# Output projection of a hybrid decoder step: low parts of the last column quarter between the additions, one-column sums between the products of the next group

## The chip, the cores and the metric

The kernel runs on one core of one Trainium2 chip. The metric is the time on the device in microseconds (us). Three runs of the kernel before gave 1358.76, 1359.56 and 1365.93 us; the median is 1359.56 us.

## The reference

One layer of a decoder works on 1088 token columns (1024 of a prompt, 64 of samples) with a width of 1024. A mixer makes two halves of 512 channels, attention heads `a` and gated groups `g`. Then:

```python
merged = concatenate([rmsnorm(a, out_norm_mla_g), rmsnorm(g, out_norm_gmlp_g)])
x = x + merged @ w_out                                   # the output projection
h2 = rmsnorm(x, norm2_g)                                 # needs the sum of x*x of each token
x = x + (silu(h2 @ w_gate) * (h2 @ w_up)) @ w_down
y = rmsnorm(x, final_norm_g)
```

All of it is in float32.

## The kernel before

Channels lie on the 128 partitions and tokens in the free dimension. Every float32 product is made of three products of rounded parts: an operand is split into a high part (`wH`, `mH`) and a low part (`wL`, `mL`, the rest), and `mm3` issues high x high, high x low and low x high (L983, L984, L985) into one PSUM accumulation.

The output projection has 16 steps i. Step i below 8 makes one block of 128 output channels for the first half of the tokens, and i from 8 for the second half; a half has two column quarters of 272 tokens. A pair (step i, column quarter c) is called a group here, and `OUT_STEPS` numbers the 32 groups by q. Group q takes 8 blocks of the contraction, so 24 products of 272 columns, into PSUM bank q % 4. Groups 0 to 15 are column quarters 0 and 1, group 16 is (8, quarter 2), group 17 is (8, quarter 3), and so on.

Who does what, each engine in the order written in its own block, tied by semaphores:

- TensorE makes the groups. From q = 4 it waits for `w_free`, the count of additions, to be q - 3 (addition q - 4 has emptied the bank), and it waits for the split of weight piece i. At group 16 it waits for all low parts (`m_lo`).
- VectorE makes the low parts `mL` of each column quarter (`mixed_low`, L2446), and adds group q to x (`add_rows`, L2458), called addition q here. Each addition waits for its group (`w_ready`) and for the x rows to be loaded. The low parts of quarter 3 (eight instructions) stand as one block between additions 3 and 4.
- ScalarE makes the high parts `mH`, and squares the new x rows (`square4`, L1879).
- GpSimd splits weight piece i (L760 the high, L763 the low part) once the group two steps back is done, and adds the squares up in `sqa` (L790). Between pieces 9 and 10 it takes the power for the factors of the first half of the tokens (L936).
- SyncE issues the transfers in one queue: weight pieces (`raw`, two buffers), x rows (`x2`; the first two loads reuse space and wait for low parts 2 and 4 of the last quarter, L632 and L634), the stores of finished x rows, and the first gate and up weights (`gate_up`, L639) with steps 8 to 11.

The sum of squares over the channels is made on TensorE with the squares as weights and a column of ones as the moving operand (`row_sums`, L1377): 6 blocks of token columns, 2 sources, and two passes for float32 operands, so 24 matmuls of one column. They stand as one clump behind group 16. VectorE makes means of them (`row_means`, L2498), GpSimd the power, VectorE diagonals (L2527), and behind group 18 TensorE spreads the factors over the partitions (L1409), which VectorE then multiplies into x (L2082).

Of the kernel before, what the change touches and what calls it, by code (L numbers as in the profile page):

```python
# [26 lines left out]
P = 128  # L27
# [5 lines left out]
KD = D // P  # L33
# [7 lines left out]
KG = GW // P  # L41
# [35 lines left out]
HALF, SUB = T // 2, T // 4  # L77
# [4 lines left out]
ADDED_1, ADDED_2 = KD - 2, 2 * KD - 5  # L82
# [20 lines left out]
def mixed_order(c):  # L103

    return MIXED if c < 3 else range(2 * KG)
# [17 lines left out]
def offsets(n):  # L123

    return [*range(0, n - P + 1, P)] + ([n - P] if n % P else [])
# [43 lines left out]
def build(nc, d):  # L169
    ctx = ExitStack()  # L170
    with ctx:
# [16 lines left out]
        ones = small.put("ones", [P, P])  # L188
# [124 lines left out]
        sqa, sqb = reg.put("sqa", [P, HALF]), reg.put("sqb", [P, 2, HALF])  # L313
# [35 lines left out]
        ps = ctx.enter_context(nc.psum_tensor("ps", [P, 8, 512], F32))  # L349
# [5 lines left out]
        def sem(name):  # L355
            return ctx.enter_context(nc.semaphore(name))
# [14 lines left out]
        nm_sq, nm_sum, nm_pick, nm_mean, nm_pow, nm_diag, nm_spread = (  # L371
            sem("nm_" + n) for n in ("sq", "sum", "pick", "mean", "pow", "diag", "spread"))
# [29 lines left out]
        m_hi, m_lo, w_ready, w_free = sem("m_hi"), sem("m_lo"), sem("w_ready"), sem("w_free")  # L402
        n4_sq, n4_added, rs_x = sem("n4_sq"), sem("n4_added"), sem("rs_x")
# [48 lines left out]
        def weights_of(t):  # L452

            k = t % TURNS
            return aHL[t % RING] if t < LAST else aHL[(LAST + k) % RING] if k < RING else aHL[k]
# [59 lines left out]
        def _(sp_):  # L515
# [96 lines left out]
            def out_piece(i):  # L612
                piece(N_OUT + i, d["w_out"][ROWS_OUT[i % KD]])

            def load_rows(j, cols=slice(0, T)):
                done = ld_uv_x if cols.start else ld_x[j]
                sp_.dma_start(x2[:, 2 * j:2 * j + 2, cols], d["x"][:, 2 * j:2 * j + 2, cols]).then_inc(done, 16)

            def keep_rows(i, c0, n, q, done):

                m = ROWS_OUT[i % KD]
                sp_.wait_ge(w_free, q + 1)
                sp_.dma_start(x2s[:, m, c0:c0 + n], x2[:, m, c0:c0 + n]).then_inc(done, 16)
# [13 lines left out]
            def gate_up(i, b):  # L637
                src = d["w_gu"][bass.ds(4 * i + b, 1), :, :].rearrange("a p n -> (a p) n")
                sp_.dma_start(wraw[:, b, :], src).then_inc(ff_full[b], 16)  # L639

            for i in range(4, 2 * KD):
                if i >= 6:
                    out_piece(i)
                if i in (6, 7):
                    load_rows(i - 6, slice(HALF, T))
                elif 8 <= i < 12:
                    gate_up(0, (2, 3, 0, 1)[i - 8])
                j = i - 4
                keep_rows(j, HALF * (j // KD), HALF, 2 * j + 1, x2_out[j // KD])
# [330 lines left out]
        def _(pe):  # L980
            def mm3(out, wh, wl, xh, xl, start, stop):

                nc.tensor.matmul(out, wh, xh, start=start, stop=False)  # L983
                nc.tensor.matmul(out, wh, xl, start=False, stop=False)  # L984
                return nc.tensor.matmul(out, wl, xh, start=False, stop=stop)  # L985
# [20 lines left out]
            for t in range(NT):  # L1006
# [4 lines left out]
                for k in range(KD):  # L1011
                    if t == 0 and k % 2 == 0:
                        pe.wait_ge(split_lo, N_V + k // 2 + 1)
                    if (c := {0: 0, 1: 1, 3: 2, 6: 3}.get(t)) is not None:

                        pe.wait_ge(n1_lo, KD * c + k + 1)
                    last = mm3(ps[0:m, b, :], hH[:, k, cols], hL[:, k, cols], vwH[:, k, :], vwL[:, k, :],
                               k == 0, k == KD - 1)
# [37 lines left out]
            for t in range(NT):  # L1056
# [7 lines left out]
                for k in range(KD):  # L1064
                    if t == 0 and k % 2 == 0:
                        pe.wait_ge(split_lo, N_U + k // 2 + 1)
                    last = mm3(ps[0:m, b, :], hH[:, k, cols], hL[:, k, cols], uwH[:, k, :], uwL[:, k, :],
                               k == 0, k == KD - 1)
# [11 lines left out]
            for m in range(KQ + KC + 1):  # L1080
                pe.wait_ge(split_lo, N_IN + m + 1)
                s = m % 2
                for c, (c0, n) in enumerate(CH):
                    q = NC * m + c
                    if q >= 4:
                        pe.wait_ge(z_free, q - 3)
                    for k in range(KD):
                        w = slice(P * k, P * k + P)
                        last = mm3(ps[:, q % 4, 0:n], wH[s][:, w], wL[s][:, w], hH[:, k, c0:c0 + n],
                                   hL[:, k, c0:c0 + n], k == 0, k == KD - 1)  # L1090
# [274 lines left out]
            for h in range(H):  # L1365
                out = ps[VH * (h % 2):VH * (h % 2) + VH, 2, NS * (h // 2):NS * (h // 2) + NS]
                for r in range(KC):
                    last = nc.tensor.matmul(out, uvr[:, r, VH * h:VH * h + VH], olat[:, r, NS * h:NS * h + NS],
                                            start=r == 0, stop=r == KC - 1)
            last.then_inc(a4, 1)  # L1370


            def row_sums(g, bank, sources, at):

                for i, o in enumerate(at):
                    for x, src in enumerate(sources):
                        last = nc.tensor.matmul(ps[:, bank, 500 + i:501 + i], src[:, o:o + P], ones[:, 0:1],  # L1377
                                                start=x == 0, stop=x == len(sources) - 1)
                last.then_inc(nm_sum, 1)

            for q, (i, c) in enumerate(OUT_STEPS):
                s = i % 2
                pe.wait_ge(split_lo, N_OUT + i + 1)
                if q >= 4:
                    pe.wait_ge(w_free, q - 3)
                elif q == 1:
                    sum_squares(J_N3 + NC - 1, 6, sqm, KG, CH[NC - 1][1])
                elif q == 2:
                    pe.wait_ge(a4_e, 1)
                elif q == 3:  # L1390
                    spread(J_N3 + NC - 1, 6, CH[NC - 1][1])
                if q == 2 * KD:
                    pe.wait_ge(m_lo, 2 * KG * 4)
                for j, k in enumerate(mixed_order(c)):
                    if i == 0:
                        pe.wait_ge(m_lo, 2 * KG * c + j + 1)
                    w, cols = slice(P * k, P * k + P), slice(SUB * c, SUB * c + SUB)
                    last = mm3(ps[:, q % 4, 0:SUB], wH[s][:, w], wL[s][:, w], mH[:, k, cols], mL[:, k, cols],
                               j == 0, j == 2 * KG - 1)
                last.then_inc(w_ready, 1)  # L1400
                if q == 2 * KD:
                    pe.wait_ge(n4_sq, KD)
                    pe.wait_ge(n4_added, ADDED_1)
                    row_sums(0, 4, (sqa[:, :], sqb[:, 1, :]), [SUB * x + o for x in range(2) for o in offsets(SUB)])
                elif q == 2 * KD + 2:
                    pe.wait_ge(nm_diag, J_N4 + 1)
                    for x in range(2):
                        for j, o in enumerate(offsets(SUB)):
                            last = nc.tensor.matmul(ps[:, 4 + x, o:o + P], ones[:, :], diag4[:, 3 * x + j, :],  # L1409
                                                    start=True, stop=True)  # L1410
                    last.then_inc(nm_spread, 1)
                elif q == len(OUT_STEPS) - 2:
                    pe.wait_ge(n4_sq, 2 * KD)
                    pe.wait_ge(n4_added, ADDED_2 + 1)
                    row_sums(1, 6, (sqa[:, :], sqb[:, 1, :]), offsets(SUB))
# [102 lines left out]
            for t in range(STEPS):  # L1518
# [13 lines left out]
                w, x = weights_of(t), bHL[t % RING]  # L1532
                for o in range(KH):
# [9 lines left out]
                    for s in range(2) if p < M7 else (p - M7,):  # L1543
                        cols = slice(SUB * s, SUB * s + SUB) if p < M7 else slice(0, SUB)
                        last = mm3(ps[:, 2 * o + s, 0:SUB], w[:, 0, at], w[:, 1, at], x[:, 0, cols], x[:, 1, cols],
                                   k == 0, k == TURNS - 1)
# [4 lines left out]
            for o in range(KH):  # L1551
                pe.wait_ge(n5_t, o + 1)
                for i, c in enumerate(offsets(SUB)):
                    if o == 0:
                        pe.wait_ge(y_last, KH + i + 1)
                        nc.tensor.matmul(ps[:, 1 + 2 * i, 500:501], sqy[:, 0, SUB + c:SUB + c + P], ones[:, 0:1],
                                         start=True, stop=False)
                    last = nc.tensor.matmul(ps[:, 1 + 2 * i, 500:501], sqt[:, 1, o, c:c + P], ones[:, 0:1],
                                            start=False, stop=o == KH - 1)
# [519 lines left out]
        def _(dve):  # L2079
# [80 lines left out]
            for t in range(NT + 1):  # L2160
# [17 lines left out]
                if t >= 1:  # L2178
                    w = t - 1
                    m, x = rows(w), v_tile(w)  # L2180
# [258 lines left out]
            def mixed_low(c, js):  # L2439

                cols = slice(SUB * c, SUB * c + SUB)
                for j in js:
                    k = mixed_order(c)[j]
                    x, gain = (aT, g_mla) if k < KG else (gT, g_gmlp)
                    dve.wait_ge(m_hi, 2 * KG * c + j + 1)
                    nc.vector.scalar_tensor_tensor(mL[:, k, cols], x[:, k % KG, cols], gain[:, k % KG:k % KG + 1],  # L2446
                                                   mH[:, k, cols], ALU.mult, ALU.subtract).then_inc(m_lo, 1)

            def add_rows(q):

                i, c = OUT_STEPS[q]
                m = ROWS_OUT[i % KD]
                x = x2[:, m, SUB * c:SUB * c + SUB]
                dve.wait_ge(ld_x[m // 2], 32)
                if m < KH and c >= 2:
                    dve.wait_ge(ld_uv_x, 48)
                dve.wait_ge(w_ready, q + 1)
                nc.vector.tensor_tensor(x, x, ps[:, q % 4, 0:SUB], ALU.add).then_inc(w_free, 1)  # L2458
# [8 lines left out]
            mixed_low(2, range(KG, 2 * KG))  # L2467
            add_rows(2)
            add_rows(3)
            mixed_low(3, range(2 * KG))  # L2470
            for q in range(4, 2 * KD + 1):
                add_rows(q)

            def weight_sums(i):

# [495 lines left out]
```

## Time and profile before

| | |
|---|---|
| median of the runs | 1359.56 us |
| profiled execution | 1362.44 us |
| its span, first to last instruction | 1360.7 us |
| TensorE busy | 1308.5 us, 96% |
| VectorE busy | 821.2 us, 60% |
| ScalarE busy | 513.0 us, 38% |
| GpSimd busy | 429.2 us, 32% |
| mean granted clock of TensorE | 0.986 |

PE is TensorE (PEld its weight loads), DVE is VectorE, ACT ScalarE, POOL GpSimd, SPq the queue of SyncE. A granted clock of 1.00 is 2.4 GHz, 0.50 is 1.2 GHz. The output projection stands at 514 to 628 us of the span. A row of the order of time gives start, duration, engine, line, operation, out<-in with shapes, the count of merged instructions, and in brackets how long the engine had been idle and who released it.

### The profile page before, as it was taken

The page shows a single profiled execution, that of the slowest core. Times are in us where ns is not written, and L with a number is a line of the kernel's source. Part 1 is how long each engine was busy: PE and PEld are TensorE (multiplying, and loading weights), DVE is VectorE, ACT ScalarE, POOL GpSimd, SP SyncE. Part 2 cuts the span into 40 slices and gives each one's busy share as a digit, 9 for nine tenths or more (in the row PEclk, how much of TensorE's full clock was granted, in tenths as well). Part 3 has the DMA queues.
Part 4 walks back from the last instruction along what each step waited for, and adds up shares of the span by engine and source line. Part 5 has one row for each costly group of instructions (what it writes and reads, how often), then busy time and mean ns, then how long its engine had stood idle before and what let it go on. Part 6 is the DMA issues. An engine that isn't in the chain of part 4 may idle for free.

```text
span 1360.7 us, 23850 instructions
## 1 busy us (share of the span) xinstructions
PE 1308.5 (96%) x9362; PEld 1226.2 (90%) x9362; DVE 821.2 (60%) x1241; ACT 513.0 (38%) x902; POOL 429.2 (32%) x279
## 2 busy tenths in 40 slices
PE   6999999999999998999999999999999999999997
PEld 4788988888888558999899999999999999999987
DVE  4874056666666338167944553445535468899976
ACT  5423224566566414113422222222222234444451
POOL 2633335442433115652044444444443400000000
PEclk9999999999999899899999999999999999999998
DMA  8421101000015444641212222122222189757503
GB/s 286 160 60 31 36 17 58 20 17 5 16 66 191 155 163 155 222 133 49 67 69 80 79 74 83 63 79 79 86 73 74 68 304 339 259 189 246 173 1 131
DMA packets 70345, 151.58 MB, mean 111 GB/s; under 512 B 9106, under 2 KB 16658, under 8 KB 69810
## 3 DMA queue, kind: packets, MB, share of 16 engines
q1 hardware_dynamic: 70258, 150.39, 32.4%
q8 instruction: 58, 0.95, 0.3%
q14 instruction: 29, 0.24, 0.1%
HBM read 127.80 MB, written 22.56 MB: 111 GB/s over the span
## 4 chain that ended last, share of the span: by engine, by line
PE 80%; DVE 8%; issue 5%; DMA 3%; ACT 2%; POOL 2%; SPq 0%; POOLq 0%; DVEq 0%; ACTq 0%
PE ps L983 24%; PE ps L984 24%; PE ps L985 24%; PE ps L1199 2%; DMA araw<-in_w_dn 2%; PE ps L1265 1%; DVE x L2082 1%; PE ps L991 1%; DMA ab<-acts 1%; PE ps L1310 1%; POOL rt L782 1%; DVE mL L2446 1%; DVE hL L2136 1%; PE ps L1275 1%; DVE aHL L2757 0%
## 5 line engine op out<-in xcount | busy, mean ns | idle before, releaser
L952 POOL TENSOR_TENSOR ws<-wraw,ws 128x1024 fp32r<-128x1024 f32 x50 | 125.2, 2504 | 215.8 <-ACT ws L1568 215.8
L983 PE MATMUL ps<-bHL,aHL 128*128 128x272 f32 x616 | 178.7, 290 | 6.3 <-DVE bHL L2760 6.1
L985 PE MATMUL ps<-bHL,aHL 128*128 128x272 f32 x616 | 177.3, 288 | 0.0
L984 PE MATMUL ps<-bHL,aHL 128*128 128x272 f32 x616 | 177.2, 288 | 0.0
L2603 DVE TENSOR_TENSOR bufP<-bufP,ps 128x544 f32<-128x544 f32 x66 | 47.4, 721 | 133.7 <-PE ps L985 131.4
L1568 ACT ACTIVATE ws<-wraw 128x1024 fp32r<-128x1024 f32 x55 | 58.4, 1061 | 174.2 <-PE ps L985 168.9
L983 PEld LDWEIGHTS ps<-bHL,aHL 128*128 128x128 f32 x616 | 116.0, 188 | 8.1 <-DVE bHL L2760 8.0
L984 PEld LDWEIGHTS ps<-bHL,aHL 128*128 128x128 f32 x616 | 116.0, 188 | 0.0
L985 PEld LDWEIGHTS ps<-bHL,aHL 128*128 128x128 f32 x616 | 116.0, 188 | 0.0
L975 POOL TENSOR_TENSOR rt<-ms,mhalf 128x3 f32<-128x3 f32 (+1 forms) x3 | 3.0, 998 | 255.1 <-DVE ms L2790 255.1
L2336 DVE TENSOR_TENSOR pTL<-ps,pTH 128x512 fp32r<-128x512 f32 (+1 forms) x96 | 53.2, 555 | 44.3 <-ACT pTH L1568 43.4
L1568 ACT ACTIVATE aHL<-araw 128x512 fp32r<-128x512 f32 x66 | 41.7, 632 | 99.4 <-PE ps L985 57.4
L952 POOL TENSOR_TENSOR ws<-wsum,ws 128x1024 fp32r<-128x1024 f32 x20 | 57.2, 2859 | 61.1 <-ACT ws L1568 61.1
L892 POOL TENSOR_TENSOR prob<-prob,rsm 128x128 f32<-128x128 f32 (+5 forms) x48 | 49.6, 1040 | 78.4 <-DVE rsm L2311 78.4
L2603 DVE TENSOR_TENSOR bufC<-bufP,ps 128x544 f32<-128x544 f32 x42 | 30.2, 720 | 70.0 <-PE ps L985 70.0
L1568 ACT ACTIVATE pTH<-ps 128x512 fp32r<-128x512 f32 (+1 forms) x96 | 46.8, 489 | 50.0 <-PE ps L1199 49.1
L1736 ACT ACTIVATE prob<-ps,nmx 128x128 f32<-128x128 f32 (+3 forms) x64 | 47.3, 740 | 24.1 <-DVE nmx L2322 23.9
L2322 DVE TENSOR_REDUCE nmx<-ps 128x1 f32<-128x128 f32 (+3 forms) x64 | 47.7, 751 | 12.7 <-PE ps L1180 12.2
L1199 PE MATMUL ps<-ident,prob 128*128 128x128 f32 x288 | 49.9, 285 | 3.0 <-DVE pTL L2336 1.8
L983 PE MATMUL ps<-x1H,ws 128*128 128x272 f32 x176 | 50.8, 288 | 2.1 <-POOL ws L952 2.1
L983 PE MATMUL ps<-x5H,ws 128*128 128x272 f32 x176 | 50.9, 289 | 1.9 <-DVE x5L L2518 1.6
L983 PE MATMUL ps<-x3H,ws 128*128 128x272 f32 x176 | 50.9, 289 | 0.9 <-DVE x3L L2513 0.9
(371 smaller groups left out, 4521.3 us busy)
## 6 DMA issues: line engine op xcount, KB each, us to landing
araw<-in_w_dn SPq DMA_DIRECT2D x121, 256.0 KB, 3.6
wraw<-in_w_gu SPq DMA_DIRECT2D x44, 512.0 KB, 3.5
cp<-in_cache SPq DMA_DIRECT2D x64, 272.0 KB, 4.5
ab<-acts SPq DMA_DIRECT2D x34, 272.0 KB, 4.5
raw<-in_w_out SPq DMA_DIRECT2D x16, 512.0 KB, 4.1
acts<-bufC SPq DMA_DIRECT2D x22, 272.0 KB, 2.1
xt<-in_x_tok SPq DMA_DIRECT2D x9, 512.0 KB, 6.7
x<-x2s SPq DMA_DIRECT2D x8, 544.0 KB, 6.1
```

The costliest lines, as they stand in the source:

```text
L782: pool.tensor_tensor(rt[:, j % 4, :], ms[:, j % 4, :], mhalf[:, :].broadcast_to((P, 3)), ALU.pow).then_inc(nm_pow, 1)
L892: pool.tensor_tensor(row, row, rsm[:, r % 4:r % 4 + 1].broadcast_to((P, n)), ALU.mult).then_inc(s_pn, 1)
L952: pool.tensor_tensor(w[:, 1, :], w_source(j), w[:, 0, :], ALU.subtract).then_inc(cw_lo, 1)
L983: nc.tensor.matmul(out, wh, xh, start=start, stop=False)
L984: nc.tensor.matmul(out, wh, xl, start=False, stop=False)
L985: return nc.tensor.matmul(out, wl, xh, start=False, stop=stop)
L1199: last = nc.tensor.transpose(ps[:, 4 + x % 2, P * qi:P * qi + P], prob[:, at:at + P], ident[:, :])
L1568: return nc.scalar.activation(out, x, ACT.Copy, scale=scale)
L1736: nc.scalar.activation(prob[:, prob_at(qt):prob_at(qt) + n], psf[:, 1024 * (r % 2):1024 * (r % 2) + n], ACT.Exp, bias=nmx[:, s:s + 1], sca ...
L2322: nc.vector.tensor_reduce(nmx[:, s], psf[:, at:at + P * (qt + 1)], AX.X, ALU.max, negate=True).then_inc(s_nm, 1)
L2336: nc.vector.tensor_tensor(pTL[:, x % 4, c0:512], ps[:, 4 + x % 2, c0:512], pTH[:, x % 4, c0:512], ALU.subtract).then_inc(t_free, 1)
L2603: nc.vector.tensor_tensor(halves(out[:, g, :]), halves(x[:, g, :]), pair(b + 2 * g), ALU.add).then_inc(added, 1)
```

## The change

The eight low parts of quarter 3 are dealt out: two behind addition 4, two behind addition 5, one each behind additions 6, 7, 8 and 9. SyncE gets a wait for all low parts before each of the gate and up loads of steps 8 to 11. The 24 one-column matmuls, behind group 16 before, are issued in group 17: behind each of the first six of its eight contraction blocks (three products each) come the four matmuls of one token block. The spreading matmuls move from behind group 18 to behind group 19.

```diff
@@ SyncE @@
                 elif 8 <= i < 12:
+                    sp_.wait_ge(m_lo, 2 * KG * 4)
                     gate_up(0, (2, 3, 0, 1)[i - 8])
@@ TensorE @@
+            def row_sum(bank, sources, i, o):
+
+                for x, src in enumerate(sources):
+                    last = nc.tensor.matmul(ps[:, bank, 500 + i:501 + i], src[:, o:o + P], ones[:, 0:1],
+                                            start=x == 0, stop=x == len(sources) - 1)
+                return last
+
             def row_sums(g, bank, sources, at):
 
                 for i, o in enumerate(at):
-                    for x, src in enumerate(sources):
-                        last = nc.tensor.matmul(ps[:, bank, 500 + i:501 + i], src[:, o:o + P], ones[:, 0:1],
-                                                start=x == 0, stop=x == len(sources) - 1)
+                    last = row_sum(bank, sources, i, o)
                 last.then_inc(nm_sum, 1)
+
+            half_at = [SUB * x + o for x in range(2) for o in offsets(SUB)]
...
                     last = mm3(ps[:, q % 4, 0:SUB], wH[s][:, w], wL[s][:, w], mH[:, k, cols], mL[:, k, cols],
                                j == 0, j == 2 * KG - 1)
+                    if q == 2 * KD + 1 and j < len(half_at):
+                        if j == 0:
+                            pe.wait_ge(n4_sq, KD)
+                            pe.wait_ge(n4_added, ADDED_1)
+                        summed = row_sum(4, (sqa[:, :], sqb[:, 1, :]), j, half_at[j])
+                        if j == len(half_at) - 1:
+                            summed.then_inc(nm_sum, 1)
                 last.then_inc(w_ready, 1)
-                if q == 2 * KD:
-                    pe.wait_ge(n4_sq, KD)
-                    pe.wait_ge(n4_added, ADDED_1)
-                    row_sums(0, 4, (sqa[:, :], sqb[:, 1, :]), [SUB * x + o for x in range(2) for o in offsets(SUB)])
-                elif q == 2 * KD + 2:
+                if q == 2 * KD + 3:
                     pe.wait_ge(nm_diag, J_N4 + 1)
@@ VectorE @@
             add_rows(3)
-            mixed_low(3, range(2 * KG))
             for q in range(4, 2 * KD + 1):
                 add_rows(q)
+                mixed_low(3, {4: (0, 1), 5: (2, 3), 6: (4,), 7: (5,), 8: (6,), 9: (7,)}.get(q, ()))
```

## Rows read from the trace of the kernel before

**Rows 1.** The page: busy time of TensorE among the engines, granted clock in 40 slices.

```profile
PE 1308.5 (96%) x9362; PEld 1226.2 (90%) x9362; DVE 821.2 (60%) x1241; ACT 513.0 (38%) x902; POOL 429.2 (32%) x279
...
PEclk9999999999999899899999999999999999999998
```

**Rows 2.** Waits between 510 and 650: us in total, times, longest.

```profile
PE ps L983 <- DVE x L2458: 4.5, 1, 4.5
```

**Rows 3.** TensorE in order of time, around the border of groups 7 and 8.

```profile
541.51 0.29 PE L985 MATMUL ps<-mH,w1L 128*128 128x272 f32 x1
546.26 0.57 PE L983 MATMUL ps<-mH,w0H 128*128 128x272 f32 x1 [4.46 <-DVE x L2458]
```

**Rows 4.** VectorE in order of time.

```profile
535.47 5.78 DVE L2446 SCALAR_TENSOR_TENSOR mL<-aT,g_mla,mH 128x272 fp32r<-128x272 f32 x4
541.18 4.59 DVE L2446 SCALAR_TENSOR_TENSOR mL<-gT,g_gmlp,mH 128x272 fp32r<-128x272 f32 x4
545.69 1.47 DVE L2458 TENSOR_TENSOR x<-x,ps 128x272 f32<-128x272 f32 x4
552.15 0.44 DVE L2458 TENSOR_TENSOR x<-x,ps 128x272 f32<-128x272 f32 x1 [4.99 <-PE ps L985]
555.21 0.44 DVE L2458 TENSOR_TENSOR x<-x,ps 128x272 f32<-128x272 f32 x1 [2.62 <-PE ps L985]
...
576.39 0.44 DVE L2458 TENSOR_TENSOR x<-x,ps 128x272 f32<-128x272 f32 x1 [2.60 <-PE ps L985]
...
583.59 0.44 DVE L2458 TENSOR_TENSOR x<-x,ps 128x272 f32<-128x272 f32 x1 [4.53 <-PE ps L985]
...
591.29 2.85 DVE L2082 SCALAR_TENSOR_TENSOR x<-x,g,ps 128x544 f32<-128x544 f32 x4
```

**Rows 5.** Stretches: length, busy time (instructions) by engine, TensorE's clock, DMA share, GB/s.

```profile
541.50:546.30 4.80, 0.34 (x4) 0.14 (x2) 4.80 (x6) 0.00 (x0) 3.50 (x2) 0.88 0.82 246
546.30:552.00 5.70, 5.70 (x25) 5.70 (x26) 0.86 (x3) 1.32 (x2) 2.68 (x2) 0.50 1.02 399
552.00:576.00 24.00, 24.00 (x193) 24.00 (x191) 3.50 (x8) 2.63 (x4) 16.88 (x11) 1.00 0.54 181
576.10:578.70 2.60, 2.60 (x26) 2.60 (x25) 0.44 (x1) 0.00 (x0) 0.75 (x1) 1.00 0.29 73
578.70:583.20 4.50, 4.50 (x26) 4.50 (x25) 0.17 (x1) 0.00 (x0) 1.34 (x1) 0.62 0.69 264
583.20:586.20 3.00, 3.00 (x26) 3.00 (x25) 1.83 (x2) 0.66 (x1) 2.54 (x2) 1.00 0.00 0
...
497.40:500.80 3.40, 2.63 (x21) 2.22 (x19) 1.92 (x4) 1.17 (x4) 0.00 (x0) 1.00 0.00 0
```

**Rows 6.** TensorE in order of time, start and end of the clump.

```profile
576.12 0.28 PE L1377 MATMUL ps<-ones,sqa 128*128 128x1 f32 x2
...
578.72 0.37 PE L983 MATMUL ps<-mH,w0H 128*128 128x272 f32 x1
578.93 0.29 PE L984 MATMUL ps<-mL,w0H 128*128 128x272 f32 x1
```

**Rows 7.** The line of the one-column sums: ns minimum/median/maximum, first and last start.

```profile
L1377 PEld LDWEIGHTS ps<-ones,sqa x24: 187/192/193, 576.0 to 631.5; 128*128 128x128 f32 x24
L1377 PE MATMUL ps<-ones,sqa x24: 164/250/251, 576.1 to 631.5; 128*128 128x1 f32 x24
```

**Rows 8.** Low parts between 530 and 550, same columns.

```profile
L2446 DVE SCALAR_TENSOR_TENSOR mL<-aT,g_mla,mH x8: 487/895/2628, 531.1 to 539.7; 128x272 fp32r<-128x272 f32 x8
```

**Rows 9.** SyncE's queue in order of time, and landing time of the pieces.

```profile
541.28 0.37 SPq L617 DMA_DIRECT2D x<-in_x  x1
...
542.91 0.48 SPq L520 DMA_DIRECT2D raw<-in_w_out  x1
...
raw<-in_w_out SPq DMA_DIRECT2D x9, 512.0 KB, 4.0
```

**Rows 10.** GpSimd in order of time.

```profile
543.07 2.40 POOL L763 TENSOR_TENSOR w1L<-raw,w1H 128x1024 fp32r<-128x1024 f32 x1
...
579.14 1.34 POOL L936 TENSOR_TENSOR rt<-ms,mhalf 128x6 f32<-128x6 f32 x1 [2.29 <-DVE ms L2498]
```

## Prediction

> **What bounds the kernel now.** I read the busy table and the clock line first. TensorE is busy 96% of the span and its clock stands at 9 tenths or more in every slice, with an 8 at slice 16 [rows 1]: time is won only where TensorE stands still, works at the lower clock, or does something other than 272-column products. The waits of the output projection come next. TensorE waits once there, 4.5 us, for an addition of VectorE [rows 2]; everywhere else VectorE waits for TensorE. The order of time on TensorE shows the place: the last product of group 7 starts at 541.51, the first of group 8 at 546.26 [rows 3]. VectorE's order gives the cause. Between 535.47 and 545.77 it makes the eight low parts of the last column quarter, and only behind them, at 545.69, the addition that frees group 8's bank, though group 4, which it adds, had ended some 13 us earlier (541.6 less three groups of 3.03, worked out below) [rows 3, 4]. Last I cut the time into stretches with the clock. After the standstill TensorE makes 25 products in 5.70 us at granted clock 0.50 (1.2 GHz), where in 552 to 576 it makes 193 in 24 us at 1.00 (2.4 GHz) [rows 5]. A second such place is the clump of one-column sums behind group 16: during it the clock is 1.00, in the 4.50 us behind it 0.62 [rows 5]. So each of the two edits meets one place where TensorE first does little and then pays in clock.
>
> **A normal group.** Additions 9 and 16 start at 555.21 and 576.39: seven groups in 21.18 us, 3.03 us each, 0.126 us for each of its 24 products [rows 4]. An addition starts 0.27 us behind the moment at which the next matmul would start (576.12 to 576.39) [rows 4, 6].
>
> **Edit 1, the low parts dealt out.** Removed: the standstill. Group 8 could start at 541.51 + 0.13 = 541.64 and starts at 546.26: 4.62 us [rows 3]. Its own length, from first product to addition 8, is 552.15 - 546.26 = 5.89 us where 3.03 + 0.27 = 3.30 would do: 2.59 us for the low clock [rows 3, 4]. Together 7.21 us. No instruction is added on TensorE or VectorE; the same eight low parts and additions 4 to 9 come in another order.
> Is the cover there? A low part takes 0.49 us alone and up to 2.63 us [rows 8], the last of them beside GpSimd's subtraction of 543.07 to 545.47 [rows 10]. An addition, which reads PSUM, took 0.44 us at 583.59 [rows 4], in a stretch where GpSimd worked [rows 5]. With addition 4 at 535.5, two lows reach 537.1, addition 5 ends near 537.5, lows 2 and 3 near 541.2, addition 6 near 541.6, low 4 and addition 7 (its group ends 541.6) near 542.5. Group 9 needs addition 5 at 544.7, group 10 addition 6 at 547.7, group 11 addition 7 at 550.7: 5 to 8 us of room, more than the worst low. Low 7 comes after addition 9, near 549, and group 16 needs it at 566. The Trainium skill's page "SBUF — State Buffer" (its part on engine ports) states that VectorE and GpSimd lock a shared pair of ports for a whole instruction when VectorE has two SBUF inputs; the rows of long lows agree. By it the additions, with one PSUM input, are not held up; were they, each would be up to 2.6 us late, still inside that room.
> SyncE's queue: its two loads of x rows wait for low parts 2 and 4. The second was issued at 541.28, just behind the fourth low, and the weight piece 6 behind it at 542.91 [rows 9]. Both lows keep their times within 0.5 us by the order above, since only two additions of about 0.4 us slip in while GpSimd is what holds the lows. What is late next: piece 6 lands 4.0 us after issue at the median [rows 9], at 547; I allow 1.5 more, 548.4, since the transfers are dense there [rows 5]. GpSimd splits it in about 3.5 us (a copy and a subtraction of 2.40 [rows 10]) from the end of group 9, now 547.7, and may have 2.8 us of square additions ahead (two of about 1.4), until 548.3. That ends near 551.9, and group 12 needs it at 553.7: about 2 us of room. Piece 5 is split by 545.47 [rows 10], group 10 needs it at 547.7. The new wait of SyncE for all low parts, ahead of the first gate piece, stands behind piece 8, which itself waits for split 6 at 551.9; the last low is there by 549. Nothing. So edit 1 gives 7.2 us; its bounds are 4.6 (clock still falls) and 7.2, less 2.6 if one low part more than shown delays piece 6.
>
> **Edit 2, the sums dealt out.** The clump is 24 matmuls (six sums, two sources, two passes each). From its first start to the second product behind it 578.93 - 576.12 = 2.81 us, less one product 2.68 us, 0.112 each [rows 6]. Additions 16 and 17 lie 7.20 us apart [rows 4]; 7.20 - 3.03 - 2.68 leaves 1.49 us, the lower clock behind the clump, 0.62 in the mean of 4.5 us [rows 5]. What does dealing do to the 2.68? A one-column matmul is over at once, what takes the time is its weight load (0.192 us each, overlapping [rows 7]). A load can lie beneath a running 272-column product, but those products have loads of their own. If every third is followed by the four matmuls of a sum, one of the five loads from it to the next product lies beneath it, as one does at the clump's start, and four are bare: 24 bare loads as before, 2.68 us. Lower bound: 48 loads of 0.108 us ((578.72 - 576.12)/24) back to back are 5.2 us against 3.03, so 2.15. Upper bound: each load and matmul one after the other, 24 x (0.192 + 0.250) = 10.6 [rows 7]. I take 2.68: the same 24 instructions in the clump row are nearest.
> And the clock? Dealt out, a stretch holds three products of 0.126 and four bare loads, 0.83 us in all, nearly half of it products. The trace has a poorer stretch that kept 1.00: 497.4 to 500.8, with 21 matmuls in 3.4 us and TensorE busy for 2.63 of them [rows 5]. So I expect 1.00 and the 1.49 us won. Bounds 0 and 1.49.
> The rest of the edit: the sums are done near the sixth of eight products' rounds, about 0.8 us before group 17 ends. VectorE's means take some 0.2, GpSimd's power 1.34 us [rows 10]; it ends some 0.8 us after group 17, and GpSimd's split 10 starts that much later. It ended 2.9 us ahead of need before; about 2 are left. The diagonals on VectorE (some 1.5 us) finish near 2.3 us after group 17, the spreading matmuls now stand behind group 19, 6 us after group 17. They cost what they did, some 1.3 us, in another place. VectorE's scaling started at 591.29 [rows 4], behind addition 19; now group 19 ends those 1.3 us sooner and the spread follows it, so the scaling's start against group 20 is unchanged within 0.3 us. ScalarE's square 8 waits for the sums' count and for addition 17; the latter stays last.
>
> **The sum.** 7.21 + 1.49 = 8.70 us. Does it come through to the end? What follows hangs on local events (spread, bank, split), each moved with TensorE; between additions 21 and 31 VectorE is busy most of the time, but from the scaling on, which moves too. The profiled execution took 1362.44 us, its span 1360.7: 1353.7 for it. The median of the runs shown, 1359.56, is 2.9 us less than that execution. The low-clock terms (2.59 + 1.49) are the ones most likely to be smaller in another execution, since the kernel has only a few such stretches; I assign them about half of the 2.9 as absent in the median run, so the change finds 7.2 there: 1352.4.
>
> **Rivals.**
> (a) The wait moves: a low part slips, load and piece 6 come later, and group 12 waits for GpSimd's split. One low of 2.63 us too many takes away some 0.6 to 2.6 us: about 1354.5. For it: GpSimd keeps the lows at 2.6; against: 2 us of room. Chance 0.12.
> (b) The clock falls in group 17 all the same: the 1.49 is not won, and the thinner group takes longer; 1354 to 1355. For it: the clump did it; against: the poorer stretch at 1.00. Chance 0.12.
> (c) The dealt loads hide. The Trainium skill's "TensorE: Matmul & The Clock Gate" (Part 2, step 1) says that TensorE pulls weight loads ahead beneath running matmuls. Worked out from the rows, as a mechanism of this kernel: loads back to back set group 17 to 5.2 us, the sums cost 2.15 and the time is 0.5 us lower, 1351.9. The page by itself would let one expect more, all 2.68; the rows' load spacing does not. Chance 0.08.
> (d) Slower: alternating one-column and 272-column products makes each load and each matmul wait for the other. At 0.44 us for each of 24 this is 10.6 us, 7.9 more than now, which eats edit 1; if this thin filling also drops the clock through groups 17 to 19 (three times 2.4 us), the time is 1359.56 - 7.2 + 7.9 + 7.2 = 1367.5. Without the clock it decides from (2.68 + 7.2)/24 = 0.41 us per dealt matmul. For it: the sums' operands are of another type than the products', and the order changes over six times instead of once; against: at the clump's borders, the same alternation, the spacing shows 0.21 against 0.13 only once [rows 6]. Chance 0.02.
>
> **How the numbers follow.** Forecast 0.66, 1352.4. The range takes the terms' bounds: low 1349.5 (all 8.7 on the median and a little more), high 1356.5 (standstill gone alone, with part of it turned into a wait for the split). 0.5%, what a measurement can tell from no change, is 6.8 us: 1352.8. The forecast lies just below that, so it splits 0.47 to 0.19; (c) counts as faster, (a) and (b) mostly as within. Faster 0.56, within 0.42, slower 0.02.
>
> **What would show it.** TensorE's order: group 8 directly behind group 7, no wait of 4.5 us, clock 1.00 from 541 to 548. Additions 16 to 17 about 5.7 us apart, 24 one-column matmuls in six clusters of four with 0.112 us between, clock 1.00 behind. VectorE: low parts in pairs between additions 4 and 6. Wrong would be a wait of TensorE for GpSimd's split at groups 10 or 12, the clock at 0.50 in group 18, or the additions 16 and 17 more than 6.5 us apart.

## Result and profile after

| | before | changed |
|---|---|---|
| median | 1359.16 us (8 runs) | 1352.63 us (8 runs) |
| lowest to highest | 1357.11 to 1365.93 us | 1348.71 to 1354.30 us |
| profiled execution, its span | 1362.44, 1360.7 us | 1352.70, 1351.0 us |

The ratio is 0.9938, 95% interval 0.9917 to 0.9959: faster by 6.5 us at the medians. The forecast was 1352.4 us.

The page after, against [rows 1]. The slice of 544 to 578, at 0.8 before, is at 0.9 now; TensorE is busy 3.5 us less and makes as many instructions.

```profile
PE 1305.0 (97%) x9362; PEld 1222.5 (90%) x9362; DVE 823.8 (61%) x1241; ACT 513.4 (38%) x902; POOL 428.5 (32%) x279
...
PEclk9999999999999899999999999999999999999998
```

TensorE in order of time at the border of groups 7 and 8, against [rows 3]: 4.75 us from start to start there, 0.13 now. The wait of [rows 2] has gone; no wait of TensorE for an addition is left in this stage.

```profile
539.97 0.29 PE L986 MATMUL ps<-mH,w1L 128*128 128x272 f32 x1
540.10 0.29 PE L984 MATMUL ps<-mH,w0H 128*128 128x272 f32 x1
```

VectorE in order of time, against [rows 4]. Additions 2, 3 and 4 stand together from 533.24, and the low parts come behind the additions 4 to 9, one or two each; additions 16 and 17 are 5.68 us apart, not 7.20.

```profile
533.24 1.12 DVE L2469 TENSOR_TENSOR x<-x,ps 128x272 f32<-128x272 f32 x3
534.29 1.69 DVE L2457 SCALAR_TENSOR_TENSOR mL<-aT,g_mla,mH 128x272 fp32r<-128x272 f32 x2
535.90 0.42 DVE L2469 TENSOR_TENSOR x<-x,ps 128x272 f32<-128x272 f32 x1
...
539.97 0.42 DVE L2469 TENSOR_TENSOR x<-x,ps 128x272 f32<-128x272 f32 x1
...
546.80 0.51 DVE L2457 SCALAR_TENSOR_TENSOR mL<-gT,g_gmlp,mH 128x272 fp32r<-128x272 f32 x1
...
567.63 0.44 DVE L2469 TENSOR_TENSOR x<-x,ps 128x272 f32<-128x272 f32 x1 [2.60 <-PE ps L986]
572.39 0.17 DVE L2509 TENSOR_SCALAR ms<-ps 128x6 f32<-128x6 f32 x1 [4.32 <-PE ps L1377]
573.31 0.44 DVE L2469 TENSOR_TENSOR x<-x,ps 128x272 f32<-128x272 f32 x1 [0.76 <-PE ps L986]
...
580.59 2.86 DVE L2093 SCALAR_TENSOR_TENSOR x<-x,g,ps 128x544 f32<-128x544 f32 x4 [0.83 <-PE ps L1420]
583.70 0.44 DVE L2469 TENSOR_TENSOR x<-x,ps 128x272 f32<-128x272 f32 x1 [0.25 <-PE ps L986]
```

Group 17 on TensorE, its first two rounds. A round is one contraction block with its four one-column matmuls; it takes 0.82 us (568.10 to 568.92).

```profile
567.73 0.28 PE L1377 MATMUL ps<-ones,sqa 128*128 128x1 f32 x2
567.87 0.36 PE L1377 MATMUL ps<-ones,sqb 128*128 128x1 f32 x2
568.10 0.37 PE L984 MATMUL ps<-mH,w0H 128*128 128x272 f32 x1
...
568.92 0.37 PE L984 MATMUL ps<-mH,w0H 128*128 128x272 f32 x1
```

Stretches after, columns as in [rows 5]: the former standstill, group 17 with its sums, and what follows. The clock is 1.00 in all three.

```profile
540.00:547.00 7.00, 7.00 (x58) 7.00 (x57) 6.34 (x9) 0.69 (x2) 6.42 (x4) 1.00 0.82 273
...
567.70:573.20 5.50, 5.50 (x49) 5.50 (x48) 0.53 (x2) 0.00 (x0) 0.98 (x2) 1.00 0.61 178
573.20:579.00 5.80, 5.80 (x49) 5.80 (x48) 2.67 (x3) 0.66 (x1) 4.77 (x3) 1.00 0.16 63
```

**Where the 9.7 us between the two spans come from.** Before the changed region 1.5 us: additions 2 and 3 started at 534.77, now at 533.24, after a shorter stretch of low clock near 235 which has nothing to do with the change. In the region 8.8 us: addition 20 moved from 594.06 to 583.70, 10.36 us less the 1.53. After it 0.7 us go back: there is a stretch at 0.50 from 678.0 to 681.4 that the profile before does not have, while TensorE waits 0.9 us less for `bHL` (5.2 us against 6.1).

```profile
678.00:681.40 3.40, 3.40 (x17) 3.40 (x17) 2.06 (x2) 0.00 (x0) 0.69 (x1) 0.50 0.00 0
```

So 8.8 us in these two executions, where the sum said 8.70. The medians over all executions show 6.5.

### The profile page after: what moved, and what is told of

It reads as the page before. It is cut to its first block, busy times and chain, and to the rows that moved or that the text cites. A ratio compares the mean times of both kernels' runs of the same rounds, so it can differ in the third digit from the quotient of the medians.

```text
span 1351.0 us, 23850 instructions
## 1 busy us (share of the span) xinstructions
PE 1305.0 (97%) x9362; PEld 1222.5 (90%) x9362; DVE 823.8 (61%) x1241; ACT 513.4 (38%) x902; POOL 428.5 (32%) x279
## 4 chain that ended last, share of the span: by engine, by line
PE 81%; DVE 8%; issue 5%; DMA 3%; ACT 2%; POOL 1%; SPq 0%; POOLq 0%; DVEq 0%; ACTq 0%
PE ps L984 24%; PE ps L985 24%; PE ps L986 24%; PE ps L1200 2%; DMA araw<-in_w_dn 1%; PE ps L1266 1%; DVE x L2093 1%; PE ps L992 1%; DMA ab<-acts 1%; PE ps L1311 1%; POOL rt L783 1%; DVE hL L2147 1%; PE ps L1276 1%; DVE aHL L2768 0%; DVE bHL L2771 0%
```

## Experiments

Theory: each edit takes away its own place; edit 1 the standstill and the low clock behind it, edit 2 only the low clock behind the clump, since the sums' weight loads cost the same wherever they stand. Rivals: all the gain lies in one edit; the dealt loads hide; changes between the two kinds of matmul cost.

**e1, edit 1 alone** (on the kernel before):

```diff
                 elif 8 <= i < 12:
+                    sp_.wait_ge(m_lo, 2 * KG * 4)
...
-            mixed_low(3, range(2 * KG))
...
                 add_rows(q)
+                mixed_low(3, {4: (0, 1), 5: (2, 3), 6: (4,), 7: (5,), 8: (6,), 9: (7,)}.get(q, ()))
```

> The kernel before with edit 1 alone (low parts dealt out, the extra wait of SyncE). Theory (each edit removes its own place): no wait of TensorE before group 8, clock 1.00 there; additions 16 and 17 stay 7.2 us apart if the clock falls behind the clump, 5.7 if it does not; time 4.6 to 7.2 us below before, ratio 0.9947 to 0.9966. Rival A (all gain is in the low parts, dealing the sums brings nothing): as fast as the changed kernel, 0.994. Rival B (the wait moves to GpSimd's split of piece 6): TensorE waits at group 12 and the gain is under 4.6.

Measured: 1354.16 us, ratio 0.9941 (0.9918 to 0.9965). No wait before group 8. The clump is followed by the low clock, and additions 16 and 17 lie 7.21 us apart (569.47 to 576.68). Stretches of this profile:

```profile
572.60:576.00 3.40, 3.40 (x17) 3.40 (x16) 0.00 (x0) 0.00 (x0) 0.96 (x1) 0.50 0.76 290
541.00:548.00 7.00, 7.00 (x57) 7.00 (x56) 6.63 (x7) 0.66 (x1) 6.17 (x5) 1.00 0.73 226
```

Edit 1 carries most of the gain: 5.4 us at the medians. Rival B is out. Rival A cannot be told from the theory by the time (1.3 us above the median of the changed kernel in e0, with overlapping intervals); the 7.21 us speak against it.

**e2, edit 2 alone:** the sums and the spread as changed, the low parts as one block as before, without SyncE's new wait.

> The kernel before with edit 2 alone (sums dealt out in group 17). Theory: the standstill of 4.6 us before group 8 and the low clock behind it stay; additions 16 and 17 are 5.7 us apart, clock 1.00 behind; time 0 to 1.5 us below before (ratio 0.9989 to 1.0), depending on whether the clump would have pulled the clock down. Rival (dealing costs something of its own): slower than before by 0.5 us or more.

Measured: 1357.30 us, ratio 0.9978 (0.9959 to 0.9996). The standstill is there, 4.46 us; additions 16 and 17 are 5.69 us apart. The rival, a cost of dealing, is out. At the medians it is 2.3 us, more than the expected 0 to 1.5; the interval takes in both. Where the clock stays up, dealing itself is worth next to nothing: from addition 16 to addition 20 this profile has 16.07 us (572.50 to 588.57), and the kernel before in e7, below, with its clump, 16.11 (572.47 to 588.58).

**e7 and e9, the kernel before again**, one profile each.

> The kernel before once more, for its profile. Theory (what follows a standstill or a clump in clock is not the same in every execution): the standstill before group 8 is 4.6 us again; the low clock behind it is there for 3 to 7 us; the low clock behind the clump may be missing, then additions 16 and 17 are 5.7 apart. Rival (fixed costs): both as in the first profile, 5.9 us from first product of group 8 to addition 8 and 7.2 us between additions 16 and 17.

> The kernel before a third time, for its profile. Two profiles of before and the one with the low parts alone showed the clump of sums: additions 16 and 17 lay 7.20 and 7.21 us apart with a stretch at 0.50 behind the clump, and 5.65 without one. Theory: one of these two values again, and for the standstill an addition 8 that comes 5.9 or 5.0 us behind the first product of group 8. Rival: values in between.

Measured, one run each: 1356.83 us and 1361.06 us. The standstill was 4.46 us in both. VectorE in e7, additions 16 and 17 around the means:

```profile
572.47 0.44 DVE L2458 TENSOR_TENSOR x<-x,ps 128x272 f32<-128x272 f32 x1 [2.60 <-PE ps L985]
574.97 0.17 DVE L2498 TENSOR_SCALAR ms<-ps 128x6 f32<-128x6 f32 x1 [2.06 <-PE ps L1377]
578.12 0.44 DVE L2458 TENSOR_TENSOR x<-x,ps 128x272 f32<-128x272 f32 x1 [2.98 <-PE ps L985]
```

The two additions are 5.65 us apart, with the clump in its old place. The clock was 1.00 during and behind it in this execution:

```profile
543.40:546.60 3.20, 3.20 (x14) 3.20 (x15) 0.89 (x3) 1.32 (x2) 2.10 (x2) 0.50 1.04 412
...
572.20:574.80 2.60, 2.60 (x27) 2.60 (x25) 0.44 (x1) 0.00 (x0) 0.73 (x1) 1.00 0.31 72
574.80:578.00 3.20, 3.20 (x28) 3.20 (x28) 0.17 (x1) 0.00 (x0) 1.34 (x1) 1.00 0.95 350
```

What the clock costs in each profile: the time from the first product of group 8 to addition 8 less 3.30 us, and from addition 16 to 17 less 5.68. The last column is the length of a stretch at 0.50 that every profile has between 436 and 452, long before the changed region:

| profile | group 8 to addition 8 | cost | additions 16 to 17 | cost | early stretch |
|---|---|---|---|---|---|
| before, first | 5.89 | 2.59 | 7.20 | 1.5 | 10.2 |
| before, e7 | 4.84 | 1.54 | 5.65 | 0.0 | 3.4 |
| before, e9 | 5.86 | 2.56 | 7.20 | 1.5 | 10.2 |
| e1, edit 1 alone | no standstill | 0 | 7.21 | 1.5 | 10.2 |
| e2, edit 2 alone | 4.85 | 1.55 | 5.69 | 0.0 | 3.4 |
| changed | no standstill | 0 | 5.68 | 0 | 10.2 |
| e0, changed again | no standstill | 0 | 5.68 | 0 | 3.4 |

The values fall on two levels, as the theory had it. The standstill is fixed, what follows in clock is not. Of four profiles with the clump the clock fell behind it in three, and the levels go with the early stretch: the higher costs stand where it was 10.2 us long. So e0 and e2, with the short one, say little on whether dealing keeps the clock up, since it stayed up in e7 too. The changed kernel's first profile says more: its early stretch is the long one, and the clock stayed up, and so it did with the long one in e3, e5, e6 and e8 below.

**e0, the changed kernel again,** beside e1 to e3.

> The changed kernel itself once more, on the chip and beside the runs of the experiments. Theory and rivals alike: ratio to before 0.9938 within 0.002. Its stretches at the lower clock: those at 234 and 439 again, none at 541 to 548 and none behind group 17; one at 678 may or may not be there.

Measured: 1352.84 us, ratio 0.9936 (0.9915 to 0.9957), profiled span 1347.6 us. As expected at 541 to 548 and behind group 17; the stretch at 678 was missing. The early ones were at 232.7 to 239.5 and 447.7 to 451.1, not quite "234 and 439".

**e3, the block one addition later:**

```diff
-                mixed_low(3, {4: (0, 1), 5: (2, 3), 6: (4,), 7: (5,), 8: (6,), 9: (7,)}.get(q, ()))
+                mixed_low(3, range(2 * KG) if q == 4 else ())
```

> The changed kernel, but all eight low parts of quarter 3 stand as one block, behind addition 4 instead of before it. Theory (only addition 4 was late, for group 8): the block of some 10 us ends near 543.5, addition 5 comes near 543.6, and group 9 needs it at 543.3 to 543.7; a wait of at most 1 us and no fall of the clock, so within 1 us of the changed kernel, ratio 0.994 to 0.995. Rival (the dealing itself is needed, every addition behind a block stops a group): TensorE stands still for 3 us or more before group 9, and the time is that of before less the sums' part, ratio 0.998 to 1.0.

Measured: 1355.96 us, ratio 0.9965 (0.9949 to 0.9982). Neither was right. TensorE stood still before group 9 for 1.8 us, more than 1 and less than 3, and the clock stayed. VectorE, and TensorE's first product of group 9:

```profile
530.46 1.12 DVE L2469 TENSOR_TENSOR x<-x,ps 128x272 f32<-128x272 f32 x3
531.50 5.75 DVE L2457 SCALAR_TENSOR_TENSOR mL<-aT,g_mla,mH 128x272 fp32r<-128x272 f32 x4
537.18 4.68 DVE L2457 SCALAR_TENSOR_TENSOR mL<-gT,g_gmlp,mH 128x272 fp32r<-128x272 f32 x4
541.78 1.47 DVE L2469 TENSOR_TENSOR x<-x,ps 128x272 f32<-128x272 f32 x4
```

```profile
542.36 0.36 PE L984 MATMUL ps<-mH,w0H 128*128 128x272 f32 x1 [1.82 <-DVE x L2469]
```

The block takes 10.4 us; with one addition ahead of it group 8 has its bank, and group 9, which could start at 540.5, waits for the next. I had counted the block's 10 us from the start of additions 2 to 4 (533.2 to 543.5); it ends 11.4 us behind that start, since the additions themselves and slower lows come on top. In the trace moving one addition saves 2.8 of the 4.6 us and the low clock, the dealing the other 1.8. The medians of e3 and the changed kernel differ by 3.1 us, more than that. The stretches at 0.50 in e3's profile from 678.7 and from 1132.7 are not e3's own: the changed kernel's first profile has one at 678.0, e1 one at 1132.4, e2 one at 1133.8. A later wait of TensorE, between 600 and 700, for GpSimd's `ws` took 3.5 us in e3 against 2.1 and 1.0 in the two profiles of the changed kernel; whether the edit or the execution makes it longer stays open.

**e4, e6, the sums twice and dealt finer.** In e4 each round makes its sum a second time into columns that nobody reads; in e6 the first source's pair stands behind the first product of a round, the second's behind the third.

```diff
+                        row_sum(4, (sqa[:, :], sqb[:, 1, :]), j + 6, half_at[j])
                         summed = row_sum(4, (sqa[:, :], sqb[:, 1, :]), j, half_at[j])
```

> The changed kernel with every one-column sum of group 17 made twice, the second copy into PSUM columns that nobody reads; 48 one-column matmuls instead of 24. Theory (bare weight loads of 0.112 us each set the cost): additions 16 and 17 lie 5.68 + 2.68 = 8.4 us apart, at clock 1.00. Rival A (loads hide beneath products): under 7.5 us. Rival B (each change between the two kinds of matmul costs, not the load): six changes stay six, so the added cost is less than 2.0. Rival C (the clock falls when the products are so thin): more than 9 us, clock 0.50 behind.

> The changed kernel with each sum split in two pairs: the pair of the first source stands behind the first product of a round, the pair of the second source behind the third. Same 24 matmuls, 12 changes between kinds instead of 6. Theory (bare loads: a pair between two products has three loads, one of them beneath the product): additions 16 and 17 again 5.68 us apart. Rival A (a change between kinds costs 0.08 us or more): 6.2 or more. Rival B (finer dealing hides more loads): 5.2 or less.

Measured, e6: 1348.64 us (one run), additions 16 and 17 5.67 us apart (564.45 to 570.12). With the sums in twelve places instead of six the group is as long as in the changed kernel: a change between the kinds costs nothing that shows, and finer dealing hides nothing. In the rows of e6 the product behind a sum is followed by the next after 0.21 us, as at the clump's end [rows 6]; the round adds up to the same 0.82 us.

```profile
564.92 0.37 PE L1413 MATMUL ps<-mH,w0H 128*128 128x272 f32 x1
565.12 0.28 PE L1414 MATMUL ps<-ones,sqa 128*128 128x1 f32 x2
565.26 0.37 PE L1415 MATMUL ps<-mL,w0H 128*128 128x272 f32 x1
565.47 0.29 PE L1416 MATMUL ps<-mH,w0L 128*128 128x272 f32 x1
565.60 0.28 PE L1417 MATMUL ps<-ones,sqb 128*128 128x1 f32 x2
565.74 0.37 PE L1413 MATMUL ps<-mH,w0H 128*128 128x272 f32 x1
```

Measured, e4: 1361.62 us (one run), additions 16 and 17 12.76 us apart (569.21 to 581.97): rival C. While the clock was up a round took 1.28 us (570.12 to 571.40), 0.46 more than the 0.82 of the changed kernel, where four bare loads give 0.45; then the clock was 0.50 from 572.3 to 586.0, the rest of the group and most of group 18. So the theory was right on the cost of each and missed the clock.

```profile
570.12 0.37 PE L984 MATMUL ps<-mH,w0H 128*128 128x272 f32 x1
...
571.40 0.37 PE L984 MATMUL ps<-mH,w0H 128*128 128x272 f32 x1
...
575.38 0.57 PE L984 MATMUL ps<-mH,w0H 128*128 128x272 f32 x1
...
577.77 0.57 PE L984 MATMUL ps<-mH,w0H 128*128 128x272 f32 x1
```

**e5, e8, one source.** Both on the changed kernel: VectorE adds the eighth square into the sum between additions 15 and 16, so each token block needs two one-column matmuls instead of four. e8 also puts the six sums in rounds 3 to 8.

```diff
-ADDED_1, ADDED_2 = KD - 2, 2 * KD - 5
+ADDED_1, ADDED_2 = KD - 1, 2 * KD - 4
...
-                        summed = row_sum(4, (sqa[:, :], sqb[:, 1, :]), j, half_at[j])
+                        summed = row_sum(4, (sqa[:, :],), j, half_at[j])
...
+                if q == 2 * KD - 1:
+                    dve.wait_ge(n4_sq, KD)
+                    dve.wait_ge(n4_added, KD - 2)
+                    nc.vector.tensor_tensor(sqa[:, :], sqa[:, :], sqb[:, 1, :], ALU.add).then_inc(n4_added, 1)
```

> The changed kernel, but the eighth square is added into the sum on VectorE (one addition of 544 columns, 0.7 us) between additions 15 and 16, where VectorE waits for TensorE, so the token sums have one source: 12 one-column matmuls in group 17 instead of 24. Theory (bare loads): additions 16 and 17 4.34 us apart instead of 5.68; 1.3 us less than the changed kernel, ratio to before 0.9928. Rival (loads hide, or changes between kinds set the cost): 5.2 us or more apart, and the same time as the changed kernel.

> The one-source kernel with the six sums in rounds 3 to 8 of group 17 instead of 1 to 6. Theory: what the one-source kernel lost is the wait of 0.93 us in front of its first sum, because VectorE's addition of the squares took 2.86 us beside GpSimd's split instead of 0.72; 0.75 us later the addition is nearly done, so group 17 (from where group 16 would be added, 3.03 us behind addition 15) takes 4.4 to 4.7 us, the wait is under 0.3, the clock stays 1.00; ratio to before 0.992 to 0.994, some 0.5 to 1.3 us less than the changed kernel, which the interval cannot tell. Rival: the later sums make factors and split 10 late, and TensorE waits before group 20.

Measured: e5 1349.25 us, ratio 0.9924 (0.9898 to 0.9949); e8 1349.09 us, ratio 0.9925 (0.9902 to 0.9948). In e5 the new addition took 2.86 us beside GpSimd's split, delayed addition 16, and TensorE waited for it; from addition 15 to addition 17 it is 8.53 us against 8.71 in the changed kernel (564.60 to 573.31). Additions 16 and 17 are 4.53 us apart, near the 4.34 expected, but addition 16 came 0.97 us late. So the trace holds 0.2 of the 1.3 us that the theory promised, and it is luck that the ratio met the expected 0.9928. VectorE and TensorE in e5:

```profile
566.31 2.86 DVE L2487 TENSOR_TENSOR sqa<-sqa,sqb 128x544 f32<-128x544 f32 x1 [0.79 <-ACT sqb L1890]
```

```profile
569.31 0.35 PE L1377 MATMUL ps<-ones,sqa 128*128 128x1 f32 x2 [0.93 <-DVE sqa L2487]
569.53 0.37 PE L984 MATMUL ps<-mH,w0H 128*128 128x272 f32 x1
569.99 0.28 PE L1377 MATMUL ps<-ones,sqa 128*128 128x1 f32 x2
570.13 0.37 PE L984 MATMUL ps<-mH,w0H 128*128 128x272 f32 x1
```

A round takes 0.60 us, 0.22 less than the 0.82 with four sum matmuls: two times 0.11. In e8 the wait is 0.19 us, and from addition 15 to 17 it is 7.70 us (565.66 to 573.36): 1.0 us less than the changed kernel. The rival's wait before group 20 did not come: addition 20 is at 583.84, 18.2 us behind addition 15, against 19.1. The median of e8 lies 3.5 us under the changed kernel's, more than the 0.9 us that is left at addition 20, and the intervals of the ratios overlap widely. Part of the rest stands behind the changed region: from addition 31 to the end e5 takes 729.3 us and e8 728.2, the changed kernel 732.9 and 730.8 in its two profiles. The wait for `ws` named at e3 was 1.0 us in e5 and absent in e8. Whether having one source causes that is not shown.

## Why the prediction was right

- *Edit 1, the standstill.* Right: 4.62 us gone, and the order of additions and lows as worked out. With the 1.53 us shift added, addition 5 started at 537.4 and ended at 537.9 (said to end near 537.5), addition 6 started at 541.5 (541.6), addition 7 at 543.2 (542.5), the last low at 548.3 (549). The prediction's reading of the clock line was loose: [rows 1] has two slices at 0.8 ahead of the last one, the one read and an earlier one (442 to 476), which is at 0.8 after the change too.
- *What is late next.* Right in kind, a little short in size. Piece 6 was the nearest; GpSimd waited 0.43 us for it to land, and its split ended at 550.96, where group 12 starts near 552.2. The room was 1.25 us and not 2. The landing took 5.7 us from issue at 541.71, above the 5.5 that I had allowed. GpSimd's row:

```profile
547.44 1.05 POOL L761 TENSOR_SCALAR w0H<-raw 128x1024 fp32r<-128x1024 f32 x1 [0.43 <-DMA raw<-in_w_out]
548.57 2.39 POOL L764 TENSOR_TENSOR w0L<-raw,w0H 128x1024 fp32r<-128x1024 f32 x1
```

- *The low clock behind the standstill, 2.59 us.* Right for that execution and e9; e7 and e2 show that it can be 1.54. Where the standstill is gone, so is it, in all profiles.
- *Edit 2, the 24 loads at 2.68 us.* Right: 5.68 - 3.03 = 2.65 dealt out, 2.62 as a clump at full clock (e7). Dealing saves none of it; e4, e5 and e6 agree with 0.11 us for each one-column matmul. That this time is its weight load, as the prediction has it, fits, but no run has one without the other. The pull-ahead of loads that rival (c) took from the Trainium skill's "TensorE: Matmul & The Clock Gate" (Part 2, step 1) did not bring the shorter group: 5.68 us where the rival needed 5.2 or less.
- *Edit 2, the clock, 1.49 us.* Right in size, and only in the executions in which the clock falls behind the clump. That the dealing prevents the fall rests on the profiles with the long early stretch: three of three with the clump fell, none of five dealt out by four or fewer did. Why e4 falls and the changed kernel does not stays open.
- *Split 10, diagonals, spread.* Right: split 10 ended at 578.05, 2.2 us before group 20; the scaling starts 3.11 us before addition 20, 2.77 before.
- *The sum and the median.* 8.7 us said, 8.8 found between the two profiles. The step from there to the median, half of the 2.9 us taken as low clock absent in the median run, was a guess that came out near: a gain of 7.2 was said, 6.5 measured. That 1352.4 and 1352.63 lie within 0.3 us is luck in part, since more runs also moved the median of the kernel before from 1359.56 to 1359.16. The runs made beside the experiments give it ground, since each has its mean granted clock. Of 49 runs of the kernel before, 21 have 0.984 to 0.986, like the first profile (0.986), and 18 have 0.990 to 0.992, like e7 (0.991); all 16 of the changed kernel have 0.989 or more. By the table the kernel before loses 4.1 us to the low clock in the first kind and 1.5 in the second, so the change is worth 8.7 or 6.2. Runs of the two kernels with the same mean clock differ by what is not clock, which should be near the standstill's 4.6: at 0.990 the means are 1357.3 (9 runs) and 1353.0 (7), 4.3 apart, and at 0.991 they are 1357.0 (6) and 1350.4 (4), 6.6 apart, so this is a rough agreement. How much of the 2.9 us lies in the early stretches was not tested.

None of the rivals came true. What (b) describes is seen in e4, where the group is thinner.

## What to carry to other kernels

Before moving work off the engine that ends last, look for the one instruction of another engine that frees its next buffer and see what stands ahead of it in that engine's order; here the same work cost 4.5 us plus the clock in one place and nothing when dealt out. A one-column matmul cost 0.11 us wherever it stood: only fewer of them are cheaper, and where they stand matters for the clock alone. When a gain lies partly in the clock, take several profiles: here one profile showed the 1.5 us in full and another not at all.

## What the runs showed of the hardware beyond what was expected

- A clump of 24 one-column matmuls, during which TensorE counts as busy without a break, was followed by the 1.2 GHz level in three of four profiles, for 3.4 us each time. Dealt out by four it was not, in four profiles (the changed kernel, e0, e2, e3); dealt out by eight (e4) it was, for 13.7 us (572.3 to 586.0).
- VectorE's addition of two 544-column SBUF operands took 2.86 us beside a GpSimd subtraction (e5) and 0.72 alone, and low parts up to 2.63 against 0.49, while additions with one operand in PSUM kept 0.42 to 0.44 in the same stretch. The Trainium skill's "SBUF — State Buffer" (its part on engine ports) states that a VectorE instruction with two SBUF inputs contends with a GpSimd instruction that reads SBUF, and that whichever starts first holds the shared ports for its whole length. The numbers agree, and e5 shows that it moves a wait onto TensorE.
